# Hybrid DeltaNet/SSD block on Trainium2: the scan's block inverse built by doubling (32, 64, 128) in small TensorE tiles

## What is computed

```python
G = jnp.cumsum(gc, axis=-1)
decay = jnp.where(tri, jnp.exp(G[..., :, None] - G[..., None, :]), 0.0)
lmat = jnp.where(strict, jnp.einsum("cbhid,cbhjd->cbhij", kb, kc) * decay, 0.0)
uw = lax.linalg.triangular_solve(lmat + I, rhs, lower=True, unit_diagonal=True)
v_new = u_i - w_i @ S                      # the chunk's solved values
o = qg_i @ S + qk_i @ v_new
S = S * exp(gl_i) + kt_i.T @ v_new
```

## Time and profile before

| | us |
|---|---|
| median of 3 runs | 1348.26 (1347.38 to 1348.37) |
| profiled execution, device time | 1350.63 |
| profiled execution, span | 1348.9 |
| TensorE busy | 1235.6 (92%) |
| VectorE busy | 766.3 (57%) |
| ScalarE busy | 429.9 (32%) |
| GpSimd busy | 226.1 (17%) |
| granted TensorE clock, mean | 0.961 of full |

### The profile page before, as it was taken

One profiled execution on the slowest core, in us unless ns is written; L12 is line 12 of the kernel. 1 busy time (PEld: TensorE's weight loads), 2 busy tenths in 40 slices (PEclk: granted clock), 3 DMA queues, 4 the chain that ended last, 5 costly groups with the idle time before them and its releaser, 6 DMA issues.

```text
span 1348.9 us, 14714 instructions
## 1 busy us (share of the span) xinstructions
PE 1235.6 (92%) x5488; PEld 715.5 (53%) x5488; DVE 766.3 (57%) x1113; ACT 429.9 (32%) x1109; POOL 226.1 (17%) x204
## 2 busy tenths in 40 slices
PE   5999999999998999899999999971699999999992
PEld 3555545555544555589999744430444444444440
DVE  5199899887925778579888656647400101010116
ACT  6243233213111112567878545531101010010113
POOL 0300000020000021166677100000100101010112
PEclk8899999999998999999999999995799999999996
DMA  9923355442142443376766755529299999999966
GB/s 366 283 79 101 103 179 152 137 149 94 47 121 82 90 94 81 81 201 206 218 211 206 269 197 187 187 78 330 77 338 339 336 336 330 343 323 352 319 221 187
DMA packets 206165, 270.69 MB, mean 201 GB/s; under 512 B 73686, under 2 KB 122831, under 8 KB 206095
## 3 DMA queue, kind: packets, MB, share of 16 engines
q1 hardware_dynamic: 186182, 212.54, 47.9%
q0 software_dynamic: 13840, 50.86, 12.3%
q10 hardware_dynamic: 6072, 6.35, 1.4%
HBM read 217.75 MB, written 51.97 MB: 200 GB/s over the span
## 4 chain that ended last, share of the span: by engine, by line
PE 75%; DVE 12%; DMA 7%; SPq 3%; ACT 2%; issue 1%; POOLq 0%; DVEq 0%; ACTq 0%
PE ps L2015 19%; PE ps L1200 16%; PE ps L1223 8%; PE ps L1155 8%; PE ps L448 4%; PE ps L429 4%; DVE arena L2382 3%; DMA arena<-ada_w 2%; DVE arena L2453 2%; DVE arena L2451 2%; DMA arena<-w_in 2%; PE ps L1914 1%; PE ps L522 1%; PE ps L495 1%; DMA tok_dram<-arena 1%
## 5 line engine op out<-in xcount | busy, mean ns | idle before, releaser
L2015 PE MATMUL ps<-arena 128*128 128x512 f32 (+1 forms) x1072 | 426.2, 556 | 5.2 <-DMA arena<-w_in 5.2
L2015 PEld LDWEIGHTS ps<-arena 128*128 128x128 f32 x1072 | 202.6, 192 | 206.3 <-issue 195.9
L1200 PE MATMUL ps<-arena 128*128 128x512 f32 x512 | 226.9, 597 | 1.4 <-ACT arena L1345 1.4
L2382 DVE SCALAR_TENSOR_TENSOR arena<-arena,taps 128x1024 f32<-128x1024 f32 x160 | 207.4, 1296 | 5.5
L1200 PEld LDWEIGHTS ps<-arena 128*128 128x128 f32 x512 | 96.7, 192 | 116.5 <-issue 114.7
L1533 DVE TENSOR_TENSOR arena<-arena,ps 128x512 f32<-128x512 f32 x16 | 11.0, 688 | 223.3 <-PE ps L1200 223.3
L1155 PE MATMUL ps<-arena 128*128 128x512 f32 x256 | 117.2, 605 | 2.4 <-DMA arena<-w_out 2.0
L1223 PE MATMUL ps<-arena 128*128 128x512 f32 x256 | 112.5, 593 | 0.0
L448 PE MATMUL ps<-arena 128*128 128x128 f32 (+5 forms) x632 | 69.6, 253 | 7.6 <-DVE arena L658 3.9
L1223 PEld LDWEIGHTS ps<-arena 128*128 128x128 f32 x256 | 47.6, 190 | 54.0 <-issue 54.0
L1155 PEld LDWEIGHTS ps<-arena 128*128 128x128 f32 x256 | 47.2, 193 | 54.0 <-issue 50.5
(11 more groups left out here) (332 smaller groups left out, 1584.0 us busy)
## 6 DMA issues: line engine op xcount, KB each, us to landing
arena<-exp_w_gate SPq DMA_DIRECT2D x16, 2048.0 KB, 11.0
arena<-exp_w_up SPq DMA_DIRECT2D x16, 2048.0 KB, 9.7
arena<-exp_w_down SPq DMA_DIRECT2D x16, 2048.0 KB, 10.6
arena<-ada_w POOLq DMA_DIRECT2D x16, 1024.0 KB, 6.6
arena<-w_in SPq DMA_DIRECT2D x28, 512.0 KB, 4.6
arena<-ada_w SPq DMA_DIRECT2D x4, 2048.0 KB, 19.7
arena<-x SPq DMA_DIRECT2D x16, 512.0 KB, 6.3
arena<-g_dram SPq DMA_DIRECT2D x16, 512.0 KB, 5.5
```

What stands on the lines that cost most here:

```text
L1200: last = mm(ps[gu_bank[s] + j][:], xsT[s][:, k, :], ew[s][j][:, k, :], start=(k == 0), stop=(k == KD - 1))
L2015: last = mm(ps[3 * (m % 2) + gi][:, 0:w], wring[(m + 1) % NW][:, k, :], hT[:, k, o:o + w], start=(k == 0), stop=(k == KD - 1))
L2382: ins = v.scalar_tensor_tensor(accg, cin_l[ci % 2][:, j // 3:j // 3 + GR, j % 3:j % 3 + GW], tp[:, j:j + 1], accg, ALU.mult, ALU.add)
```

## The change

The inverse is built by doubling. `near`: for two pairs of neighbouring 32-blocks, G32 = AT.Xd (32x32 tiles). `block_pairs`: G32 times Y's diagonal blocks gives the off-diagonal block of each pair, and for one pair also its transpose, put into Xd. `block_far`: G64 = AT.Xd for the 64-block off the diagonal. `block_halves`: G64 times Y gives the last quarter. All copies, with sign, are on ScalarE (`near_out`, `pairs_out` with three instructions, `far_out`, `halves_out`); `block_p` and `block_y` are gone. `scaled_x` is gone: the step size goes into the exponent bias of the SSD decay, as ln(dt), by one extra Ln in `gates_second`. The queues are reordered: outputs and to_s go ahead of from_chunk on TensorE, new_s ahead of y_diag on VectorE, mask_ssm ahead of y_off, load_xy after load_e on SP, tail_k, far_out, decay8, halves_out at the end on ScalarE.

```diff
+        PAIRS = (((0, 1), (2, 3)), ((1, 0), (3, 2)))
+        FROM, INTO = (half(0), half(1)), (half(1), half(0))
...
+        def near(d):
             for h in range(DN_H):
+                for a, b in PAIRS[d]:
+                    last = nc.tensor.matmul(heads(bA[d][:])[quarter(b), h, 0:BL], AT[d][quarter(a), h, quarter(b)],
+                                            Xd[d][quarter(a), h, quarter(a)], start=True, stop=True)
+            return last
...
+            def block_pairs(step):
+                d, n = step
+                pe.wait_ge(sem("s_wq"), part(4, step, 1))
+                for h in range(DN_H):
+                    for a, b in PAIRS[d]:
+                        mm(heads(bA[d][:])[quarter(a), h, 0:BL], G32[d][quarter(b), h, :], Y[d][quarter(b), h, quarter(b)],
+                           start=True, stop=True)
+                a, b = PAIRS[d][d]
+                for h in range(DN_H):
+                    last = mm(heads(bA[d][:])[quarter(b), h, BL:2 * BL], Y[d][quarter(b), h, quarter(b)], G32[d][quarter(b), h, :],
+                              start=True, stop=True)
+                last.then_inc(sem("s_blk"), 1)
+
+            def block_far(step):
+                d, n = step
+                pe.wait_ge(sem("s_wq"), part(4, step, 2))
+                for h in range(DN_H):
+                    last = mm(heads(bA[d][:])[INTO[d], h, HALF:P], AT[d][FROM[d], h, INTO[d]], Xd[d][FROM[d], h, FROM[d]],
+                              start=True, stop=True)
+                last.then_inc(sem("s_blk"), 1)
+
+            def block_halves(step):
+                d, n = step
+                pe.wait_ge(sem("s_wq"), part(4, step, 3))
+                for h in range(DN_H):
+                    last = mm(heads(bA[d][:])[FROM[d], h, HALF:P], G64[d][INTO[d], h, :], Y[d][INTO[d], h, INTO[d]],
+                              start=True, stop=True)
+                last.then_inc(sem("s_blk"), 1)
...
             def solve(step):
-                pe.wait_ge(sem("s_py"), part(2, step, 2))
+                pe.wait_ge(sem("s_wq"), part(4, step, 4))
...
                 if own and nxt:
-                    block_w(nxt)
+                    block_near(nxt)
                 if lat(own):
                     from_state(own)
                 if own:
                     solve(own)
                 if nxt:
-                    block_vy(nxt)
+                    block_pairs(nxt)
+                if lat(own):
+                    outputs(own)
+                if own and own[1] < LAST:
+                    to_s(own)
+                if nxt:
+                    block_far(nxt)
                 if lat(own):
                     from_chunk(own)
-                    outputs(own)
-                if nxt:
-                    block_vp(nxt)
                 if own and own[1] < LAST:
-                    to_s(own)
                     to_state(own)
                 if nxt:
-                    block_vq(nxt)
+                    block_halves(nxt)
...
                 if nxt:
+                    near_out(nxt)
                 if own:
                     d, n = own
                     evac(heads(bB[d][:]), U[d], own, ("s_xr", turn(d, n + 1)), "s_u")
+                if nxt:
+                    pairs_out(nxt)
                 if own and two:
                     decay(act, two)
-                if lat(nxt):
-                    scaled_x(nxt)
...
                 if nxt and nxt[1] < LAST:
                     tail_k(nxt)
+                if nxt:
+                    far_out(nxt)
+                if lat(nxt):
+                    decay8(nxt)
+                if nxt:
+                    halves_out(nxt)
...
             def load_at(step):
-                    sp_.wait_ge(sem("s_blk"), part(4, (d, n - 1), 1))
+                    sp_.wait_ge(sem("s_blk"), part(4, (d, n - 1), 3))
             def load_xy(step):
-                    sp_.wait_ge(sem("s_py"), part(2, (d, n - 1), 1))
+                    sp_.wait_ge(sem("s_xr"), turn(d, n))
...
+                act.wait_ge(sem("g_act"), 6)
+                a(gb[:], sp[:], ACT.Ln, bias=tiny[:])
                 a(wtail[:], ga[:], ACT.Exp).then_inc(sem("g_act"), 1)
```

More of the change, by code:

```diff
@@ L442, in from_k, with block_near @@
                 per_head(bB[d], kgT[d], S[d]).then_inc(sem("s_ks"), 1)
[L444 to L451, removed]
+            def block_near(step):
                 d, n = step
@@ L454, in block_w @@
                 pe.wait_ge(sem(f"ld_xy{d}"), 64 * (n + 1))
[L455 to L459, removed]
+                near(d).then_inc(sem("s_blk"), 1)
+            def block_pairs(step):
                 d, n = step
[L461 to L464, removed]
@@ L518, in from_chunk @@
                 pe.wait_ge(sem("s_sc"), turn(d, nl(step) + 1))
[L519 removed]
+                x_ = heads(xtok[:, tile_of(step), :], SSM_H)
                 for h in range(SSM_H):
[L521 to L522 removed]
+                    for rows in (half(0), half(1)):
+                        last = mm(D_[rows, h * SSM_P:(h + 1) * SSM_P], E8[d][:, h, rows], x_[:, h, :],
                                   start=True, stop=True)
@@ L578, in decay8 @@
                 last.then_inc(sem("s_e8"), 1)
-            def scaled_x(step):
-                d, n = step
-                t = tile_of(step)
-                if nl(step) > 0:
-                    act.wait_ge(sem("s_fc"), turn(d, nl(step)))
-                for h in range(SSM_H):
-                    last = a(xdt[d][:, h, :], xtok[:, t, h * SSM_P:(h + 1) * SSM_P], ACT.Copy,
-                             scale=sp[:, t, d, DN_H + h:DN_H + h + 1])
-                last.then_inc(sem("s_xd"), 1)
             def tail_k(step):
@@ L601, in evac, with minus, near_out, pairs_out @@
                 a(dst, src, ACT.Copy).then_inc(sem(name), 1)
+            def minus(dst, src):
+                return a(dst, src, ACT.Copy, scale=-1.0)
+            def near_out(step):
+                d, n = step
+                evac(heads(bA[d][:])[:, :, 0:BL], G32[d], step, ("s_blk", part(4, step, 1)), "s_wq")
+            def pairs_out(step):
+                d, n = step
+                act.wait_ge(sem("s_blk"), part(4, step, 2))
+                for a_, b in PAIRS[d]:
+                    minus(Y[d][quarter(a_), :, quarter(b)], heads(bA[d][:])[quarter(a_), :, 0:BL])
+                a_, b = PAIRS[d][d]
+                minus(Xd[d][quarter(b), :, quarter(a_)], heads(bA[d][:])[quarter(b), :, BL:2 * BL]).then_inc(sem("s_wq"), 1)
+            def far_out(step):
+                d, n = step
+                evac(heads(bA[d][:])[INTO[d], :, HALF:P], G64[d][INTO[d]], step, ("s_blk", part(4, step, 3)), "s_wq")
+            def halves_out(step):
+                d, n = step
+                act.wait_ge(sem("s_blk"), part(4, step, 4))
+                minus(Y[d][FROM[d], :, INTO[d]], heads(bA[d][:])[FROM[d], :, HALF:P]).then_inc(sem("s_wq"), 1)
             for s in range(-2, 2 * NS):
@@ L900, in sp_scan @@
                     load_at(two)
-                    load_xy(two)
                 if two and two[1] > 0:
@@ L905, in sp_scan @@
                     load_e(three)
+                if two:
+                    load_xy(two)
                 if lat(two):
```

71 lines of the change are left out of this document (25 added, 46 removed).

## The result

The changed kernel took **1351.66 us** (median of 17 runs, 1346.60 to 1361.16), the kernel before beside it 1346.88 (17 runs, 1343.76 to 1350.72). The ratio is **1.0034 [1.0019, 1.0049]**: 4.8 us slower, inside the range and near the +5.4 that was forecast. Already the runs hint at it. The 17 values of the changed kernel fall into ten between 1346.6 and 1352.2, whose TensorE was granted a mean clock of 0.955 to 0.962, and seven between 1354.5 and 1361.2, with 0.948 to 0.953. The profiled execution is of the second kind: 1357.81, span 1356.1, clock 0.949.

A forecast was written before the change was run, and what follows sets the result against it. TensorE's own queue was taken to bound the latent steps. Latent steps +2.2, first steps +4.1, end -1.5 and +0.6 gave +5.4 us on the median 1348.26, so 1353.7 us, range 1342 to 1366.

The forecast's parts named there:

- Latent steps: The 14 steps from solve 4 to 18: each 10.74 us against 10.58, shape changes outweighing saved streaming, +2.2 us.
- no cost: In latent steps, outputs waits for U behind solve and pairs; claimed free, with faster pairs bringing at most 0.07 us.
- near's pace: Streaming of near's 32x32 products on TensorE, taken as 0.027 us each, 0.43 for 16.
- lower bound: 0.013 us per 32x32 product, if 32 columns stream in half the time and two tiles run side by side.
- First steps' queue: far_out behind decay and tail_k on ScalarE: solve 0 +3.0, solve 0 to 1 +0.2, solve 1 to 4 +0.9 us.
- The walk through ScalarE's queue: Adding up ScalarE's copies, decay and tail_k with halves to time the first solves; together +4.1 us.
- End: Solve 18 to 19 shortens by 1.5 us; the last step, where outputs waits for U, adds 0.6.
- A: Rival: shape changes cost nothing for small tiles, so a latent step takes 9.8 us; 1340.5 us, chance 0.24.
- B: Rival: products under 64 columns get no cheaper, so near +0.43 and pairs +0.64 us; 1372 us, chance 0.12.
- C: Rival: a late E8 transfer moves mask_ssm, decay8 and halves_out, and solve waits; 1368 us, chance 0.06.
- D: Rival: VectorE was the bound, and its 1.1 us come back in 16 steps; 1334 us, chance 0.04.
- The expected sign: Whole kernel: slower with chance 0.60, within 0.2% 0.16, faster 0.24.

The follow-up runs named there:

- e9: e4 plus, between from_state and solve of each latent step, one useless 32x32 product or, by direction, a full-width one of 32 columns; 1349.37 us, one run.
- e11: The changed kernel with its own queue order, plus useless products in TensorE's waits of the first steps; 1345.96 us, ratio 0.9973 to the kernel before.
- e12: Control: the kernel before plus useless products in its first steps, placed as in e5; 1348.54 us, ratio 0.9990.
- e7: e4 with far taken over all 128 rows, which gives it from_chunk's shape; 1345.73 us, one run.
- e8: e4 with near ahead of from_k, right behind halves; 1353.13 us, one run. The text's "late E8" means a data transfer, not this run.
- e6: The kernel before with only the step size moved into the exponent (scaled_x out, extra Ln in); 1348.97 us, ratio 0.9996.
- e1: The changed kernel with ScalarE's tail_k of step 0 behind halves_out instead of ahead of far_out; 1347.25 us, ratio 1.0002 to the kernel before.
- e4: The changed kernel with, in the first steps, far_out directly behind pairs_out and tail_k behind halves_out; 1350.97 us, ratio 1.0012 to the kernel before.
- e5: e4 plus useless 128-wide products in TensorE's short waits of the first steps; 1344.41 us, ratio 0.9969 to the kernel before.

## Why the prediction was right, and where it was not

**Right in the total, by errors that cancel.** Predicted +5.4, measured +4.8. That the two are so near is luck, as the terms show:

- **Latent steps: predicted +2.2, measured -4.6.** The mechanism was right (the step is the sum of TensorE's blocks, 10.39 for the forecast 10.74) and two sizes were off. *near* was put at 0.43 + 0.18 and took 0.37; all other blocks are within 0.03 but pairs (0.76 for 0.82). Pairs would be shorter still, 0.60, but outputs waits 0.16 for U, a wait that the prediction put at nothing ("no cost").
- **near's pace**, the first size. The rows of pairs show it: ten L475 from 691.77 to 691.93, 0.016 each. e9's small tile, whose two instructions hold TensorE for 0.18, is nearly all exit, so some 0.16 of near's 0.37 is exit too and 0.21 / 16 = 0.013 the pace. That is the prediction's lower bound (two tiles side by side); it had taken the middle. The Trainium skill, "TensorEngine Tiling (Array Packing)", "Key Properties", says that different tiles can load and multiply in parallel. The trace agrees: one tile alone would take 0.027 by block_vq's pace, and these take 0.013 to 0.016. The Trainium skill's "TensorE: Matmul & The Clock Gate", "Wait — 56ns, not 53.3ns?", has about 25 ns as the least from one start to the next. By that, near would take 16 x 0.025 + 0.16 = 0.56, an estimate; the rows show 0.37. The section does not speak of different tiles, and these rows are of different tiles.
- **The baseline**, the second size: the forecast 10.74, made of means over both directions, was set against a single step of 10.58, though the prediction also has 150.3 us for 14 steps, 10.74 each. That step has the shorter block_w (0.68, not 0.89): the steps before are 10.55 and 10.80 by turns, and the first two of the scan's latent steps 11.1 and 11.3. Mean against mean it is 10.41 for 10.74.
- **First steps' queue: predicted +3.0, +0.2 and +0.9; measured +3.1, and +0.9 for the other two together** (e11: 33.94 for 33.05). The walk through ScalarE's queue was right to 0.3 us.
- **End: predicted -1.5 and +0.6, measured -1.5 and +0.7.**
- **Not predicted: TensorE's clock in the first steps**, up to +12.6. The windows of before have PEclk beside every busy time, 1.00 in 550 to 570, and the prediction changed the work of just that stretch without asking whether the clock depends on it. Without this the terms give 3.1 + 0.9 - 4.6 - 1.5 + 0.7 = -1.4. The seven long runs of the changed kernel (median 1357.8) lie 10.9 above the kernel before, as -1.4 + 12.6 = +11.2 has it; the ten others (middle 1349.1) lie 2.2 above, so they too seem to lose 3.6 or more, which is inferred, since their windows were not recorded. e11 and e12 show that the loss is the clock's: it goes with products that do nothing from the changed kernel, and nothing that can be measured goes from the one before.

**The rivals.** A (changes of shape cost nothing for small tiles: a step of 9.8) fell: e9 shows the 0.38 and e7 the 0.15. What it had right was the 0.013. B (a floor at 64 columns) fell by the same rows, C (late E8) by the 1.5 us that halves' copy has in hand, D (VectorE was the bound) by a VectorE freed of 7.9 us in 50 while the step is still the sum of TensorE's blocks; e6 shows the same for ScalarE. The expected sign was right for a reason that was not in the text: had the clock held, this change would have been faster or within 0.2%.

**What stays open.** Which of the short waits brings the clock down, what in the new inverse keeps it down (its small tiles or its order), and why it comes back after some ten microseconds in one execution and after 45 in another, wasn't settled; e1 and e4 have the same short waits and differ in how many runs were long (1 of 10 above 1354, and 5 of 10). The parts of e11 add up to about -0.7 against the profile of before (its first product to solve 0 is 12.4, +3.9), while it measured -2.7 to -3.6 by medians and ratio. Against e6's profile, with its fall of the clock, e11's scan, 204.8 by the same two products, is 3.7 us shorter, so the missing 2 to 3 us may be what the kernel before itself loses by the clock in most of its runs; with no windows of those runs this is not shown.

## What to carry to other kernels

Read PEclk in every stretch whose TensorE work a change makes thinner or splits into small pieces, and price it as a term of its own: here it was larger than all others together, and differed from run to run. Small tiles stream cheaply (0.013 us for a 32x32) and cost by the trip (0.38 from full width and back, 0.15 between two adjoining shapes), so put products of one shape next to each other, unless what follows isn't ready. Compare a mean with a mean: where two kinds of step alternate, one step read from a timeline is not the average of the two. And take the profile of one execution as one draw: with the same first steps on TensorE the clock cost nothing in one (before) and some 3 us in another (e6).

## What the runs showed of the hardware

- TensorE's granted clock went from 1.00 to 0.50 in 550 to 560 us with waits of only 1.6, 0.9 and 0.5 us between small products (e4), and stayed at 0.50 to about 606 us while TensorE was booked for 9.3 us and more of ten. Useless full-width products in those waits kept it at 0.89 to 1.00 (e5) or 1.00 (e11, with the changed kernel's own order).
- With the inverse of the kernel before and the same waits of 1.9, 0.8 and 0.5 us, the clock stayed at 1.00 in one execution (before) and was 0.70 and 0.78 in 550 to 570 in another (e6).
- One and the same kernel gave 1341.7 and 1358.1 (e4), with mean clocks of 0.963 and 0.946. Only the longer one was profiled, so that all of the difference lies in the first steps is not shown.
- 32x32 products in different tiles that write one bank of PSUM took 0.013 to 0.016 us each (after, e9), about half of the 0.027 that block_vq's pace gives for 32 columns in one tile, so two ran side by side.
- A product of 32 columns over the whole array, put between two long ones, costs 0.22 us in all; the same in a 32x32 tile 0.38.
